# A hybrid decoder layer on eight cores: weight loads written ahead of their use, in a program that is built twice

## What is computed

```
h      = RMSNorm(x)
u_pool | u_rnn | u_gate | g_pool | g_rnn = h @ W_in      # 512, 1024, 1024, 1024, 1024 columns
y_pool = PoolMixer(u_pool) @ W_pool_out                  # causal windows 2, 4, 8, 16 in 4 groups
y_rnn  = (RG-LRU(conv4(u_rnn)) * gelu(u_gate)) @ W_rnn_out
x      = x + (sigmoid(g_pool) * y_pool + sigmoid(g_rnn) * y_rnn) @ W_o
x      = x + (silu(gate) * up) @ W_ffn_out,   gate | up = RMSNorm(x) @ W_ffn_in   # 2 x 2816 columns
out    = RMSNorm(x)
```

## Time and profile before

| | before |
|---|---|
| median of 3 runs | 1413.25 us (1409.62 to 1413.79) |
| profiled execution | 1409.78 us |
| its span, slowest core (core 1) | 1407.3 us |
| spans of the eight cores | 1389.4 to 1407.3 us |
| TensorE busy | 1061.3 us (75%) |
| VectorE busy | 847.9 us (60%) |
| ScalarE busy | 661.5 us (47%) |
| GpSimd busy | 198.9 us (14%) |
| software DMA queue (weights) | 69.88 MB, 47.5% of 16 engines |

### The profile page before, as it was taken

How to read it: one execution, slowest core, us unless ns; L and a number is a source line. 1 busy time by engine, 2 the same in 40 slices (tenths; PEclk the granted TensorE clock), 3 DMA queues, 4 the chain that set the end, 5 groups by cost and what they waited for, 6 DMA issues and landing times.

```text
span 1407.3 us, 18621 instructions; the slowest of 8 cores (1389.4 to 1407.3 us)
## 1 busy us (share of the span) xinstructions
PE 1061.3 (75%) x4720; PEld 463.2 (33%) x4720; DVE 847.9 (60%) x1380; ACT 661.5 (47%) x1039; POOL 198.9 (14%) x235
## 2 busy tenths in 40 slices
PE   1344443687554799778999998884889889999991
PEld 0112111233221344334444443331334434444440
DVE  1368878765888733445642789897523444555565
ACT  2488888887876421368322555653311341111112
POOL 2000000111000123011112211110113012121100
PEclk9867766899776899999999999997999999999996
DMA  9533323955212378469639765641787658755622
GB/s 154 115 60 61 52 45 60 204 53 51 23 19 23 31 77 89 64 88 143 62 30 103 88 58 63 68 43 53 201 95 67 89 61 99 83 67 58 71 33 118
DMA packets 241865, 106.33 MB, mean 76 GB/s; under 512 B 225376, under 2 KB 225504, under 8 KB 241760
## 3 DMA queue, kind: packets, MB, share of 16 engines
q0 software_dynamic: 222832, 69.88, 47.5%
q1 hardware_dynamic: 18928, 35.27, 7.9%
HBM read 166.60 MB, written 8.39 MB: 124 GB/s over the span
## 4 chain that ended last, share of the span: by engine, by line
PE 51%; DVE 23%; DMA 8%; ACT 8%; issue 8%; SPq 1%; DVEq 1%; ACTq 0%; POOLq 0%
PE ps L227 35%; PE ps L648 8%; DVE scr L421 5%; DVE scr L361 4%; PE ps L560 3%; PE ps L588 3%; ACT hbf L234 2%; DMA WA<-w_o 2%; DVE X L652 2%; DVE hbf L241 2%; DVE scr L419 2%; DMA xs<-xp 2%; DVE scr L393 2%; DMA ring<-w_rnn_out 1%; DMA ring<-w_in 1%
## 5 line engine op out<-in xcount | busy, mean ns | idle before, releaser
L227 PE MATMUL ps<-h2T,ring 128*128 128x512 bf16 x1568 | 371.6, 392 | 1.6 <-DVE scr L629 0.9
L227 PE MATMUL ps<-h1T,ring 128*128 128x512 bf16 x1280 | 329.3, 413 | 6.3 <-DMA ring<-w_in 5.2
L227 PEld LDWEIGHTS ps<-h2T,ring 128*128 128x128 bf16 x1568 | 157.1, 101 | 197.8 <-issue 28.2
L227 PEld LDWEIGHTS ps<-h1T,ring 128*128 128x128 bf16 x1280 | 134.5, 105 | 186.5 <-issue 60.7
L648 PE MATMUL ps<-WA,R 128*128 128x512 bf16 x704 | 171.6, 388 | 29.7 <-DVE X L652 29.7
L627 ACT ACTIVATE scr<-ps 128x512 f32<-128x512 f32 x88 | 52.4, 596 | 246.1 <-PE ps L227 233.7
L361 DVE SCALAR_TENSOR_TENSOR scr<-scr,cw 128x512 f32<-128x512 f32 x192 | 144.3, 751 | 20.5
L652 DVE SCALAR_TENSOR_TENSOR X<-ps,X 128x512 f32<-128x512 f32 x192 | 131.8, 690 | 36.0 <-PE ps L648 29.3
L220 POOL DMA_DIRECT2D ring<-w_in x92 | 80.7, 880 | 472.0 <-PE ps L227 435.9
L629 DVE SCALAR_TENSOR_TENSOR scr<-scr,ps 128x512 f32<-128x512 f32 x88 | 60.4, 686 | 133.1 <-PE ps L227 102.0
L380 PE MATMUL ps<-vb,rga 128*128 128x512 bf16 x64 | 29.6, 463 | 140.6 <-ACT vb L368 123.5
(11 more groups left out here) (84 smaller groups left out, 1217.8 us busy)
## 6 DMA issues: line engine op xcount, KB each, us to landing
ring<-w_in POOLq DMA_DIRECT2D x92, 256.0 KB, 5.4
ring<-w_ffn_in POOLq DMA_DIRECT2D x88, 256.0 KB, 6.3
xs<-xp SPq DMA_DIRECT2D x16, 512.0 KB, 5.0
xs<-xc SPq DMA_DIRECT2D x16, 512.0 KB, 4.6
X<-xc SPq DMA_DIRECT2D x16, 512.0 KB, 11.7
WA<-w_ffn_out POOLq DMA_DIRECT2D x8, 1024.0 KB, 9.2
out<-X SPq DMA_DIRECT2D x16, 512.0 KB, 2.7
ring<-w_rnn_out POOLq DMA_DIRECT2D x16, 256.0 KB, 5.6
```

The source lines that it names most:

```text
L227: S.op("pe", lambda e, bank=bank, slot=slot, kc=kc, half=half, hT=hT, K=K: e.matmul(ps[bank][:, :], lhsT=ring[:, slot, kc, :], rhs=hT[:, k ...
```

## The change

Three things are changed:

- The program is built twice. The first pass (`build_program(None)`) records the ring loads in the order of their use. The second gets that list, and `load_block` number i issues every load up to number i + 3 (`PF_D = 3`) that hasn't been issued yet. A slot counts as open from the issue of a load to `close_block`, which is called behind the last matmuls that read the block; at an open slot the pump stops. `close_block` pumps again, up to three beyond the last load used.
- The ring index is now the load's number modulo 6, which is the same rotation as before.
- `phC2` gets a part: both Squares of a pair of units are issued, then both Sqrts.

`load_wo` and `wl` are as before, at the same places of the list. The core of the diff:

```diff
+PF_D = 3
-def build_program():
+def build_program(prefetch=None):
+    load_log = []
...
-        def load_block(src, K):
-            slot = nring()
-            S.op("pool", lambda e, slot=slot, src=src, K=K: e.dma_start(out=ring[:, slot, 0:K, :], in_=src),
+        NRING = 6
+        lstate = {"emitted": 0, "use": 0}
+        open_slots = set()
+
+        def emit_load(desc, slot):
+            v, c0, K = desc
+            src = views[v][:, :, c0:c0 + 128]
+            S.op("pool", lambda e: e.dma_start(out=ring[:, slot, 0:K, :], in_=src),
                  writes=[("ring", slot)], dma_sem=("ring", slot))
-            return slot
+            open_slots.add(slot)
+
+        def pump_loads(upto):
+            while lstate["emitted"] <= min(upto, len(prefetch) - 1):
+                k = lstate["emitted"]
+                if (k % NRING) in open_slots:
+                    break
+                emit_load(prefetch[k], k % NRING)
+                lstate["emitted"] += 1
+
+        def load_block(v, c0, K):
+            desc = (v, c0, K)
+            i = lstate["use"]
+            lstate["use"] += 1
+            load_log.append(desc)
+            if prefetch is None:
...
+            else:
+                assert prefetch[i] == desc
+                pump_loads(i + PF_D)
...
+            return i % NRING
+
+        def close_block(slot):
+            open_slots.discard(slot)
+            if prefetch is not None:
+                pump_loads(lstate["use"] - 1 + PF_D)
...
-                        phC2(r - 3)
-                        phC2(r - 2)
+                        phC2(r - 3, 0)
+                        phC2(r - 2, 0)
+                        phC2(r - 3, 1)
+                        phC2(r - 2, 1)
...
         def mix_block(m, hT, hkey):
...
+                if half == 1:
+                    for sl_ in (sGP, sGR, sPO, sRO):
+                        close_block(sl_)
...
-    nc = build_program()
+    _, log = build_program(None)
+    nc, _ = build_program(log)
```

More of the change, by code:

```diff
@@ L196, in build_program @@
         cnt = {"ring": 0, "bank": 0, "ss": 0, "xs0": 0, "hbf": 0, "unit": 0, "plu": 0}
[L198 to L201, removed]
         def nbank():
@@ L216, in nunit @@
             return p
-        def load_block(src, K):
-            slot = nring()
-            S.op("pool", lambda e, slot=slot, src=src, K=K: e.dma_start(out=ring[:, slot, 0:K, :], in_=src),
-                 writes=[("ring", slot)], dma_sem=("ring", slot))
-            return slot
+        views = {"in": w_in_v, "po": w_pool_out_v, "ro": w_rnn_out_v, "fi": w_ffn_in_v}
+        NRING = 6
[5 more added lines that the diff above has]
+            S.op("pool", lambda e: e.dma_start(out=ring[:, slot, 0:K, :], in_=src),
+                 writes=[("ring", slot)], dma_sem=("ring", slot))
+            open_slots.add(slot)
[12 more added lines that the diff above has]
+            if prefetch is None:
+                assert (i % NRING) not in open_slots, "ring slot still in use"
+                emit_load(desc, i % NRING)
+            else:
+                assert prefetch[i] == desc
+                pump_loads(i + PF_D)
+                assert lstate["emitted"] > i, "load %d could not be issued: ring slot busy" % i
+            return i % NRING
[3 more added lines that the diff above has]
+                pump_loads(lstate["use"] - 1 + PF_D)
         def proj(bank, slot, hT, hkey, half, K=8):
@@ L343, in phA @@
                 if half == 0:
-                    slots[j] = load_block(w_in_v[:, :, 512 + 128 * j: 512 + 128 * (j + 1)], 8)
+                    slots[j] = load_block("in", 512 + 128 * j, 8)
                 ub, kub = bufs(u)["ub"]
@@ L347, in phA @@
                 proj(b0, slots[j], hT, hkey, half)
+                if half == 1:
+                    close_block(slots[j])
                 S.op("act", lambda e: e.activation(out=ub[:, 3:515], in_=ps[b0][:, :], func=AF.Copy),
@@ L395, in phC, with phC2 @@
                      reads=[kw, kv], writes=[kw])
-            def phC2(u):
+            def phC2(u, part):
                 B = bufs(u)
@@ L400, in phC2 @@
                 a2, ka2 = B["a2"]
[L401 to L405, removed]
+                if part == 0:
+                    S.op("act", lambda e: e.activation(out=a2[:, 0:512], in_=a[:, 0:512], func=AF.Square),
+                         reads=[ka], writes=[ka2])
+                else:
+                    S.op("act", lambda e: e.activation(out=a2[:, 0:512], in_=a2[:, 0:512], func=AF.Sqrt,
+                                                       scale=-0.25, bias=q25[:]),
+                         reads=[ka2], writes=[ka2])
             def phD(u):
@@ L460, in f @@
                     for j in (j0, j0 + 1):
-                        slot = load_block(w_in_v[:, :, 1536 + 128 * j: 1536 + 128 * (j + 1)], 8)
+                        slot = load_block("in", 1536 + 128 * j, 8)
                         for half in range(2):
@@ L464, in f @@
                             proj(b0, slot, hT, hkey, half)
+                            if half == 1:
+                                close_block(slot)
                             S.op("act", lambda e, b0=b0, j=j, half=half: e.activation(
@@ L478, in f @@
                         if g not in slots:
-                            slots[g] = load_block(w_in_v[:, :, 128 * g:128 * (g + 1)], 8)
+                            slots[g] = load_block("in", 128 * g, 8)
                         slot = slots[g]
@@ L487, in f @@
                         proj(b0, slot, hT, hkey, half)
+                        if half == halves[-1]:
+                            close_block(slot)
                         S.op("act", lambda e: e.activation(out=pb[:, 0:15], in_=ph[:, g, :], func=AF.Copy),
@@ L542, in mix_block @@
         def mix_block(m, hT, hkey):
[L543 to L546, removed]
+            sGP = load_block("in", 2560 + 128 * m, 8)
+            sGR = load_block("in", 3584 + 128 * m, 8)
+            sPO = load_block("po", 128 * m, 4)
+            sRO = load_block("ro", 128 * m, 8)
             for half in range(2):
@@ L617, in f @@
                         if half == 0:
-                            slots[i] = (load_block(w_ffn_in_v[:, :, 128 * fidx:128 * (fidx + 1)], 8),
-                                        load_block(w_ffn_in_v[:, :, D_FF + 128 * fidx:D_FF + 128 * (fidx + 1)], 8))
+                            slots[i] = (load_block("fi", 128 * fidx, 8),
+                                        load_block("fi", D_FF + 128 * fidx, 8))
                         sG, sU = slots[i]
@@ L626, in f @@
                         proj(bU, sU, hT, hkey, half)
+                        if half == 1:
+                            close_block(sG)
+                            close_block(sU)
                         S.op("act", lambda e: e.activation(out=th[:, 0:512], in_=ps[bG][:, :], func=AF.Tanh, scale=0.5),
@@ L778, in _ @@
             S.emit_engine("pe", e, sems, dsems)
-    return nc
+    return nc, load_log
 _WINDOWS = (2, 4, 8, 16)
```

## The result

The changed kernel takes 1441.07 us in the median, the kernel before 1413.09 us on the same chips. The ratio is 1.0203 (95% interval 1.0189 to 1.0217), that is 28.7 us slower (26.7 to 30.7). The forecast was 1430 with a range of 1418 to 1438: the sign was right, and the time lies outside the range.

What follows compares the result with a forecast made beforehand. The prediction took w_o's issue time to set the chain twice, with TensorE waiting on its loads. 8.3 + 10.0 + 1.6 - 1.1 = +18.8 us gave 1428.6 or 1432.1, so 1430 us, range 1418 to 1438.

Steps and rivals of the forecast that it cites:

- `wl` and the ring loads: FFN output loads go behind up to three ring loads, other ring loads go earlier: cost nothing, gain nothing.
- The ring stalls: TensorE's waits on ring loads, 5.2 + 1.9 us before: forecast to stay about the same.
- Rival D: Kernel gets faster because stalls on ring loads go: -7.1 us, and -1.1 more if w_o isn't held, 1404; chance 0.06.
- the ScalarE term: Grouped Squares and Sqrts in `phC2`: each pair 0.19 us shorter, six pairs on the chain, -1.1 us.
- the w_o terms: w_o issued behind the third FFN load, landing later by 8.3 and 10.0 us, plus 1.6 us of slow clock.
- an emptier queue: First w_o load, scaled by bytes: 15.9 us instead of 18.3, so landing 8.3 us later while issued 10.7 later.
- rival B: w_o late by its full delay, nothing repaid: 10.7 + 10.6 + 1.6 - 1.1 = 21.8 us, some 1434; chance 0.17.
- The lower bounds: Least delay of w_o's two landings: +5.4 and +8.2 us, or 0 and +2.8 if both halves land in 6.8 us.
- rival C: w_o alone is fast, both halves landing in 6.8 us: +3.3 us, 1416, or up to +13; chance 0.13.
- The slow clock: TensorE's w_o matmuls after the second stop run slower, 4.40 - 2.76 = 1.6 us; the first stop has it already.

Runs made afterwards that it cites:

- the third buffer: Kernel before with both Squares of a pair then both Sqrts, and a third a2 buffer: 1412.59 us beside 1414.85, ratio 0.9982.
- loads only: Changed kernel with Square, Sqrt, Square, Sqrt as before, loads still three ahead: 1434.82 us beside 1412.12 for the kernel before, ratio 1.0162.
- The run with the queue held: As loads only, but GpSimd issues the next ring load behind w_o only after w_o has landed: 1438.18 us beside 1414.85, ratio 1.0160.
- the single runs: One part each: loads only, 22.9 us slower than the kernel before; and the kernel before with only the Squares and Sqrts grouped, 7.6 us slower.

## Why the prediction was off

**Right.** The direction, the place of the main loss and its mechanism. w_o went behind the third FFN load, which waits for the last block's g_pool slot, both times on the chain; measured from the rnn_out load it is 10.3 us later (11.2 instead of 0.9), and against the mixer's last matmul 10.6 us both times on the mean of the cores, where 10.7 and 10.6 were forecast. `wl` and the ring loads cost nothing: `wl` is issued at 1184.10, and its first reader runs at 1208.43. The ring stalls stayed (7.4 before, 6.8 after), since the slots and not the list held the loads back. Rival D had no room.

**Wrong: the ScalarE term, -1.1 us.** The step said that no instruction is added and that "a pair gets 0.19 us shorter". It timed the moved Square by its own durations and never asked what it writes. Measured: +7.6 us (4.7 to 10.6), by 23.5 us of waits on the scan, which the third buffer takes away. This step alone moves the sum by 8.7 us. The row that would have shown it stands in VectorE's timeline of the kernel before:

```profile
127.27 1.28 DVE L421 TENSOR_TENSOR_SCAN scr<-scr,hst 128x512 f32<-128x512 f32 x1
```

That scan ends at 128.55. The second Square ran at 129.89, 1.3 us clear of it, and moved up behind the first it would start at 127.8 (127.27 + 0.62 - 0.09), in the middle of it.

**Undersized: the w_o terms, 8.3 + 10.0 + 1.6 = 19.9 us.** Measured: 22.9 us (19.5 to 26.1), an interval that takes in 19.9, so the time alone doesn't show the terms wrong. The traces do, by 2.8 us. The kernel with loads only beside before, on the mean of the cores, from the end of the mixer's last matmul, first and second load of w_o:

| us from the mixer's last matmul | before | loads only | growth |
|---|---|---|---|
| w_o's first half issued | -13.5, -13.5 | -2.9, -2.9 | 10.6, 10.6 |
| w_o's second half landed | 3.4, 2.5 | 13.3, 12.5 | 9.9, 10.0 |
| 17th matmul with W_o starts | 7.1, 5.6 | 18.3, 17.1 | 11.2, 11.5 |

The last row sums to 22.7 us, which is the whole measured loss. The landing of the second load was right (10.0). That of the first was forecast at 8.3 and is 9.9: the step took back 2.4 us for an emptier queue, by bytes, and the queue behind w_o doesn't slow it down (15.0 and 15.1 us with and without that queue empty). It also took one FFN load behind w_o where there were three. The 0.7 us by which w_o is faster than before (15.1 beside 15.7) are within what runs of the same order differ by (15.7, 16.3, 17.0).

The rule that the prediction named beside this step, from the Trainium skill ("DMA: Bandwidth & Descriptors", "Two DMAs through the same engine are not ordered"), is that descriptors in one queue of one DMA engine start in order. The run with the queue held agrees with it, and so do the packets of the kernel before. Its sum was rival B's upper bound, 10.7 + 10.6 + 1.6 = 22.9, the measured value to the digit. That match is partly luck: B has the landings too late by 1.4 us and the slow clock too small by 1.2. The prediction held against the rule that 3.0 MB had moved where 2.5 MB had to be through. The window of the earlier trace rows ends at 572, so it counts 0.18 MB moved behind 571 and the FFN packets of the last 3 us, shown above. The lower bounds and rival C took the 6.8 us of the earlier trace rows for a half of w_o. It is an FFN load of three column blocks (768 KB); the fastest load of 1024 KB in that trace took 8.7 us.

**The slow clock, sized at 1.6 us.** On the slowest cores of the changed kernel the second stop adds 4.28 - 2.76 = 1.5 us, as sized. The first, which the prediction left at its old cost, adds 5.29 - 4.40 = 0.9 us more. With loads only, on the mean of the cores, both together are some 2.8 us (the last row of the table less the one above).

**Sum.** 22.9 + 7.6 = 30.5 us from the single runs, 28.7 measured together; the intervals cover the difference. The sizes of the two waits are shown by removing each. What put the time outside the range is the ScalarE term: without its 8.7 us the measured 1441 would be some 1432, inside it.

## What to carry to other kernels

A prefetch written into an in-order issue queue gains nothing where buffer slots already let that queue run ahead, and it costs wherever it puts a load that must wait ahead of one that is needed first. So list the queue as it will be, with what each entry waits for, and not the source. For a moved instruction ask what it writes and who still reads that buffer, also where nothing is added and each duration is known: with two buffers, earlier by 2 us can be too early. Where a large load is on the chain, its place is worth more than the depth of the small ones: moving w_o alone gave 9.5 us.

## What the runs showed of the hardware

A 2.1 MB load in a queue of small ones takes nearly the same time whatever is behind it (15.0 and 15.1 us from the issue of its second half, without and with three 0.26 MB loads there). It takes longer by what is ahead (18.2 us behind two FFN loads of 0.26 MB issued within 2.2 us before it, 15.7 to 17.0 us in the three runs that have only mixer weights there). The loads behind it moved next to nothing until its last 3 us (at most 16 of 843 packets from 558 to 568 us in the kernel before, 1270 of 1389 in the 3 us behind). The clock of TensorE fell to 1.2 GHz during the 9 us wait itself (0.70, then 0.50 in the windows from 574 us), so that the first half's four matmuls took 1.86 us instead of 1.02; here they lie in the wait for the second half and cost nothing.
